# A two-layer decoder trunk with expert gathers: stream place in halves, VectorE work moved, two loads split by rows, fifteen tiny loads at the end

## What is computed

```python
def peer_ffn(h, w_q, sub_keys, u_tab, v_tab):
    q = (xt @ w_q).reshape(T, PEER_HEADS, 2, PEER_HALF)
    s = jnp.einsum('thpd,hpkd->thpk', q, sub_keys)
    s_top, i_top = lax.top_k(s, PEER_TOPK)              # 16 of 128, twice per head
    best, pos = lax.top_k(cand, PEER_TOPK)              # 16 of the 256 sums
    gates = jax.nn.softmax(best, axis=-1)
    act = jnp.einsum('chkd,cd->chk', u_tab[ib], xb)
    act = jax.nn.gelu(act) * gb
    return jnp.einsum('chk,chkd->cd', act, v_tab[ib])

for i in range(DEPTH):
    h = h + (diff_attention if i == 0 else short_conv)(rmsnorm(h, norm_mix[i]), ...)
    h = h + peer_ffn(rmsnorm(h, norm_ffn[i]), ...)
```

## Time and profile before

| | us |
|---|---|
| median of three runs | 1553.16 (1553.01 to 1554.8) |
| the profiled execution | 1554.41 |
| its span, first to last instruction | 1552.6 |
| TensorE busy | 1345.4 (87%) |
| VectorE busy | 1005.9 (65%) |
| ScalarE busy | 594.2 (38%) |
| GpSimd busy | 583.1 (38%) |
| moved by DMA | 626.06 MB, mean 403 GB/s |

### The profile page before, as it was taken

The page is one execution under the profiler, slowest core; times in us unless marked ns, Lnnn a source line. Parts: engine busy times, 40 slices in busy tenths (PEclk is TensorE's granted clock), DMA queues, the critical chain, the costliest instruction groups (busy, mean ns, idle before and its releaser), DMA issues.

```text
span 1552.6 us, 13146 instructions
## 1 busy us (share of the span) xinstructions
PE 1345.4 (87%) x3288; PEld 571.5 (37%) x3288; DVE 1005.9 (65%) x2452; ACT 594.2 (38%) x1809; POOL 583.1 (38%) x516
## 2 busy tenths in 40 slices
PE   8899898899868899988887889999888898777777
PEld 3454343344323443333332334344333333322222
DVE  5677877677566975445478636666548867765454
ACT  1334354534332444333334424343434344343333
POOL 0023334344323343333335444343344444444341
PEclk9999999999999999999999999999999999999999
DMA  9659999999999999999999999999999999999996
GB/s 395 247 230 418 419 415 414 420 365 420 418 422 419 372 418 420 418 421 420 419 420 420 417 421 421 420 419 420 420 417 389 423 421 421 421 421 422 420 422 281
DMA packets 92810, 626.06 MB, mean 403 GB/s; under 512 B 10304, under 2 KB 10432, under 8 KB 25152
## 3 DMA queue, kind: packets, MB, share of 16 engines
q0 software_dynamic: 73728, 536.90, 83.6%
q1 hardware_dynamic: 17280, 81.01, 12.9%
q10 hardware_dynamic: 1728, 7.31, 1.2%
HBM read 624.14 MB, written 1.05 MB: 403 GB/s over the span
## 4 chain that ended last, share of the span: by engine, by line
DMA 44%; PE 35%; DVE 12%; ACT 5%; issue 3%; POOL 0%; ACTq 0%; SPq 0%; DVEq 0%; POOLq 0%
DMA ring<-in_peer_uv_dram,idx 43%; PE acc L600 23%; PE pp L360 9%; DVE ring L1353 5%; ACT diag L915 1%; PE tt L375 1%; PE acc L360 1%; ACT weight L911 1%; DMA ring<-in_w_qkv_dram 1%; PE ss L434 1%; ACT gelu L909 1%; ACT L909 1%; ACT rows L737 1%; DVE mx L1022 0%; ACT L774 0%
## 5 line engine op out<-in xcount | busy, mean ns | idle before, releaser
L600 PE MATMUL acc<-ring,diag 128*128 128x512 f32 x2048 | 988.7, 609 | 153.0 <-ACT diag L915 142.3
L695 POOL DMA_INDIRECT ring<-in_peer_uv_dram,idx x512 | 582.9, 1139 | 948.8 <-PE acc L600 830.3
L1353 DVE CUSTOM_DVE_ANT_0 ring<-ring,xf 128x1024 f32<-128x1024 f32 x512 | 627.0, 1227 | 469.9 <-DMA ring<-in_peer_uv_dram,idx 459.0
L600 PEld LDWEIGHTS acc<-ring,diag 128*128 128x128 f32 x2048 | 372.1, 192 | 701.4 <-issue 688.4
L909 ACT ACTIVATE gelu<-dots 128x1 f32<-128x1 f32 x512 | 103.6, 202 | 816.9 <-DVE dots L1353 816.7
L915 ACT ACTIVATE diag<-const,weight 128x128 f32<-128x128 f32 x512 | 205.5, 401 | 17.2
L911 ACT ACTIVATE weight<-gelu,gates 128x1 f32<-128x1 f32 x512 | 150.7, 294 | 17.0
L360 PE MATMUL pp<-stream,xT 128*128 128x512 f32 x160 | 80.5, 593 | 0.0
L360 PE MATMUL pp<-stream,rows 128*128 128x512 f32 x128 | 65.9, 597 | 0.0
L360 PEld LDWEIGHTS pp<-stream,xT 128*128 128x128 f32 x160 | 30.2, 190 | 37.7 <-issue 37.7
L375 PE MATMUL tt<-const,rows 128*128 128x128 f32 x144 | 23.6, 287 | 21.5 <-ACT rows L708 15.7
(11 more groups left out here) (139 smaller groups left out, 746.9 us busy)
## 6 DMA issues: line engine op xcount, KB each, us to landing
stream<-in_peer_w_q_dram SPq DMA_DIRECT2D x36, 512.0 KB
stream<-in_conv_w_in_dram SPq DMA_DIRECT2D x32, 512.0 KB
stream<-in_w_qkv_dram SPq DMA_DIRECT2D x16, 512.0 KB
ring<-in_peer_uv_dram,idx POOLq DMA_INDIRECT x512
ring<-in_w_qkv_dram SPq DMA_DIRECT2D x3, 2048.0 KB, 24.2
stream<-in_w_o_dram SPq DMA_DIRECT2D x8, 512.0 KB
kept<-in_peer_w_q_dram SPq DMA_DIRECT2D x2, 2048.0 KB, 11.9
stream<-in_conv_w_out_dram SPq DMA_DIRECT2D x8, 512.0 KB
```

The costliest lines, as they stand in the source:

```text
L600: mm = nc.tensor.matmul(acc[half][:, :], diag[:, s % RING, :], row[:, D + half * 512:D + (half + 1) * 512], start=(k == 0), stop=(k == SLO ...
L695: nc.gpsimd.indirect_dma_start(dst, None, uv_dram, bass.IndirectOffsetOnAxis(idx[:, at:at + 1], 0)).then_inc(landed, 16)
L1353: nc.vector.tensor_tensor_reduce(row[:, 0:D], row[:, 0:D], xf[:, s // SLOTS % 2, :], 1.0, 0.0, ALU.mult, ALU.add, dots[:, s % RING:s % RIN ...
```

## The change

The stream place is filled in two halves of four k steps in place of four quarters of two. Of window 1's queries the third and fourth chunk are projected at slots 120 and 134 and not at 116 and 128; of window 0's the last at 51 and not 57; of window 3's the first at slot 88 of its count and not 90, and it is ranked one step a slot and not two. `scale_for_mixer` and `scale_for_experts` get a `yield` between the sum of squares and the root, with a tile of their own (`total`) for the sum, and the former starts four slots later. The two kept chunks named above are loaded as rows 0 to 119 and rows 120 to 127, and TensorE waits for both. Fifteen loads of i rows (i = 1 to 15) of 16 + i columns of the constants into a used part of `kept` are issued by SP after slot 506 has been used, ahead of its output stores, and waited for at the end.

```diff
@@ AT
-         wq0=94, wq1=104, wq2=116, wq3=128),
+         wq0=94, wq1=104, wq2=120, wq3=134),
@@
-         scale=86, wq0=90, wq1=106, wq2=132, wq3=156),
+         scale=86, wq0=88, wq1=106, wq2=132, wq3=156),
-LATE_RANK_PROJECT = {1: 0, 2: 25, 3: 57}
+LATE_RANK_PROJECT = {1: 0, 2: 25, 3: 51}
-RANK_PIECES = {(0, 1): 2, (0, 2): 2, (0, 3): 1, (1, 0): 2, (3, 0): 2}
+RANK_PIECES = {(0, 1): 2, (0, 2): 2, (0, 3): 1, (1, 0): 2}
-QUARTERS = 4
+FIFTEEN = {(2, "in", 2), (2, "out", 0)}
+MOST = 120
+PARTS = 2
+DEEP = KT // PARTS
@@ wait_weights
-                    if k % 2 == 0:
-                        pe.wait_ge(quarter_in[k // 2], 16 * (before + 1))
+                    if k % DEEP == 0:
+                        pe.wait_ge(part_in[k // DEEP], 16 * (before + 1))
                 elif k == 0:
                     pe.wait_ge(w_in[place], 16 * (before + 1))
+                    if (n, what, c) in FIFTEEN:
+                        pe.wait_ge(rest_in[(n, what, c)], 16)
@@ load_stream
-                size = KT // QUARTERS * CHUNK
-                for q in range(QUARTERS):
-                    if previous is not None and q < QUARTERS - 1:
-                        sp.wait_ge(quarter_used, (QUARTERS - 1) * (before - 1) + q + 1)
+                size = DEEP * CHUNK
+                for part in range(PARTS):
+                    if previous is not None and part < PARTS - 1:
+                        sp.wait_ge(part_used, (PARTS - 1) * (before - 1) + part + 1)
@@ the loads
+                    if (n, what, c) in FIFTEEN:
+                        sp.dma_start(places[place][0:MOST, :], matrix_of(n, what, c)[0:MOST, :]).then_inc(w_in[place], 16)
+                        sp.dma_start(places[place][MOST:P, :], matrix_of(n, what, c)[MOST:P, :]).then_inc(rest_in[(n, what, c)], 16)
+                    else:
+                        sp.dma_start(places[place], matrix_of(n, what, c)).then_inc(w_in[place], 16)
                 previous[place] = n, what, c
+            written(sp, pp, (3, "out", 0))
+            sp.wait_ge(v_used, ALL - 5)
+            for i in range(1, 16):
+                sp.dma_start(kept[0:i, 1, 64 * i:64 * i + 16 + i], consts[0:i, 0:16 + i]).then_inc(small_in[i - 1], 16)
             for b in range(2):
                 for c in range(2 - b):
                     sp.wait_ge(h_finished, 2 * (2 + b) + c + 1)
                     sp.dma_start(out_dram[b][:, c * CHUNK:(c + 1) * CHUNK], h[:, b, c * CHUNK:(c + 1) * CHUNK]).then_inc(out_done, 16)
+            for i in range(1, 16):
+                sp.wait_ge(small_in[i - 1], 16)
             sp.wait_ge(out_done, 64)
@@ scale_for_mixer, and the same in scale_for_experts
                 sum_squares(n % 2)
+                yield
                 rsqrt_of_mean(1, D, scale_mix[:, n:n + 1])
@@ output
                 yield at["scale"]
-                scale_for_experts(n)
+                yield from paced(scale_for_experts(n), at["scale"], 1)
@@ gated_input
-                yield at["x"]
-                scale_for_mixer(n)
+                yield at["x"] + 4
+                yield from paced(scale_for_mixer(n), at["x"] + 4, 1)
                 if n == 2:
-                    yield at["x"] + 2
+                    yield at["x"] + 7
```

More of the change, by code:

```diff
@@ L196, in build @@
         stat = sb("stat", [P, 8])
+        total = sb("total", [P, 1])
         root = sb("root", [P, 8])
@@ L228, in build @@
         w_first_in = [sem("w_first_in0"), sem("w_first_in1")]
-        quarter_in = [sem(f"quarter_in{i}") for i in range(QUARTERS)]
-        quarter_used = sem("quarter_used")
+        part_in = [sem(f"part_in{i}") for i in range(PARTS)]
+        part_used = sem("part_used")
+        rest_in = {(2, "in", 2): sem("rest_in0"), (2, "out", 0): sem("rest_in1")}
+        small_in = [sem("small_in%d" % i) for i in range(1, 16)]
         v_first_used = sem("v_first_used")
@@ L362, in project_part @@
                         mm.then_inc(pool.written_sem(key), 1)
-                    elif k % 2 and held(n, what, c)[0] == STREAM:
-                        mm.then_inc(quarter_used, 1)
+                    elif k % DEEP == DEEP - 1 and held(n, what, c)[0] == STREAM:
+                        mm.then_inc(part_used, 1)
             def project(pool, n, what, c, src, at, ks=range(KT)):
@@ L640, in load_stream @@
             def load_stream(n, what, c, before, previous):
-                size = KT // QUARTERS * CHUNK
-                for q in range(QUARTERS):
-                    if previous is not None and q < QUARTERS - 1:
-                        sp.wait_ge(quarter_used, (QUARTERS - 1) * (before - 1) + q + 1)
+                size = DEEP * CHUNK
+                for part in range(PARTS):
+                    if previous is not None and part < PARTS - 1:
+                        sp.wait_ge(part_used, (PARTS - 1) * (before - 1) + part + 1)
                     elif previous is not None:
                         written(sp, pp, last_reader(*previous))
-                    sp.dma_start(stream[:, q * size:(q + 1) * size],
-                                 matrix_of(n, what, c)[:, q * size:(q + 1) * size]).then_inc(quarter_in[q], 16)
+                    sp.dma_start(stream[:, part * size:(part + 1) * size],
+                                 matrix_of(n, what, c)[:, part * size:(part + 1) * size]).then_inc(part_in[part], 16)
             load_first()
@@ L661, in _ @@
                         written(sp, values_pool(1), (1, "values", 1))
-                    sp.dma_start(places[place], matrix_of(n, what, c)).then_inc(w_in[place], 16)
+                    if (n, what, c) in FIFTEEN:
[3 more added lines that the diff above has]
+                        sp.dma_start(places[place], matrix_of(n, what, c)).then_inc(w_in[place], 16)
                 previous[place] = n, what, c
+            written(sp, pp, (3, "out", 0))
+            sp.wait_ge(v_used, ALL - 5)
+            for i in range(1, 16):
+                sp.dma_start(kept[0:i, 1, 64 * i:64 * i + 16 + i], consts[0:i, 0:16 + i]).then_inc(small_in[i - 1], 16)
             for b in range(2):
@@ L940, in rsqrt_of_mean @@
             def rsqrt_of_mean(count, dim, y):
-                v, t = stat[:, 0:count], root_t[:, 0:count]
+                v, t = stat[:, 0:count] if count > 1 else total[:, :], root_t[:, 0:count]
                 link(nc.vector.tensor_scalar(v, v, 1.0 / dim, EPS, ALU.mult, ALU.add))
@@ L955, in sum_squares @@
             def sum_squares(b):
-                link(nc.vector.tensor_tensor_reduce(scratch[:, 0:D], h[:, b, :], h[:, b, :], 1.0, 0.0, ALU.mult, ALU.add, stat[:, 0:1]))
+                link(nc.vector.tensor_tensor_reduce(scratch[:, 0:D], h[:, b, :], h[:, b, :], 1.0, 0.0, ALU.mult, ALU.add, total[:, :]))
             def square_groups(src3, count, dim, sq):
@@ L1215, in front @@
                 dve.wait_ge(x_in[0], 16)
-                scale_for_mixer(0)
+                whole(scale_for_mixer(0))
                 prepare_gains()
@@ L1236, in front @@
                 dve.wait_ge(x_in[1], 16)
-                scale_for_mixer(1)
+                whole(scale_for_mixer(1))
                 add_output(0, 0)
                 add_output(0, 1)
-                scale_for_experts(0)
+                whole(scale_for_experts(0))
                 expert_rows(0)
```

## The result

The changed kernel takes 1566.48 us at the median (1565.17 to 1567.11) against 1553.54 for the kernel before in the same comparison: 1.0077 times as long, 95% interval 1.0064 to 1.0089. I had forecast 1543.5, and a range that ended at 1553. The change is slower by 13 us, and none of my rivals is the reason: that rival 2 names 1567 is chance, since its mechanism (late halves) is not what the trace shows.

What follows compares the result with a forecast made beforehand. The prediction took DMA transfers, 626 MB at 421 GB/s, plus idle time of the DMA engines as the bound. Terms -3 -3.5 -1 -1 +2 -2 -1.2 summed to -9.7 us, from 1553.16 to 1543.5 us; range 1535 to 1553.

Steps and rivals of the forecast that it cites:

- rival 2: Streamed halves land late where chunks' slots adjoin, so TensorE waits; 1567 us, or 1556 at 1 us each; chance 0.07.
- the first two dips: Transfer rate drops in slice 9 (365 GB/s, 5.1 us lost) and slice 14 (372 GB/s, 4.4 us lost).
- the third: Transfer rate drop in slice 31 (389 GB/s), 2.9 us lost.
- the tail: Last slots' loads from 1538 us: one of sixteen engines some 5 us behind, and every slot waits for it.
- (a): Streamed place in halves: 50 loads of 1 MB instead of 100 of 512 KB, -3 us (0 to -4.4).
- (b): VectorE in slots 129 to 136 (slice 14): scale split and later, rankings overlap less; -3.5 us (0 to -4.4).
- (e): TensorE in slots 134 to 141: late query projection beside the input chunk lengthens slots; +2 us (0 to +5).
- (c): Window 0's heads 6 and 7 projected at slot 51 instead of 57 (slice 9); -1 us (-5.1 to +3).
- (d): Window 3's first heads ranked one step a slot, project two slots earlier (slice 31); -1 us (0 to -2.9).
- (g): SP's end: window 2's two stores moved to the last slots, fifteen tiny issues hidden before the last store; -1.2 us.
- rival 3: SP's fifteen tiny issues hold up the last store; 1570 us at 2.35 us an issue; chance 0.04.
- (f): Two kept chunks loaded as 120 + 8 rows, sparing an engine that may be the lagging one; -2 us (-5 to +1.2).

Runs made afterwards that it cites:

- experiment 7: Changed kernel with whole kept loads, varied: streamed place in quarters 1550.12 us; steps at old slots, scales in one piece 1550.96; without tiny loads, stores early 1548.21, late 1547.54.
- experiment 6: Changed kernel with whole kept loads, its fifteen tiny loads replaced by five of 1, 2, 3, 8 and 16 rows, each followed by a marker load: 1546.23 us.

## Why the prediction was wrong, point by point

**What bounds the kernel: right.** What was won and lost stands in the GB/s lines: the first two dips gave some, the third and the tail nothing, and about half a rate for some 35 us was the place where the time was lost.

**(a) Halves: right in direction, the size within the noise.** Forecast -3, measured -3.0 with about 3 us of uncertainty. The rows of the kernel with whole loads show how: SP's queue takes 12.7% for 81.02 MB, 0.1567% a MB, where it was 0.1592%; the gathers have 0.1565%.

```profile
q0 software_dynamic: 73728, 536.90, 84.0%
q1 hardware_dynamic: 10320, 81.02, 12.7%
```

The packets say it more finely: from 120 to 1500 us, one of 4 KB on SP's queue took 0.163 us on average in the kernel before, and one of 8 KB 0.316 in this one, 3% less than two of the former. On the 52.4 MB streamed, 124 us at 421 GB/s, that is an estimate of some 3.6 us.

The shorter lead (rival 2) shows once, and costs next to nothing. The page's rows of the kernel before and of this one, busy us, mean ns, idle before:

```profile
L360 PE MATMUL pp<-stream,xT 128*128 128x512 f32 x160 | 80.5, 593 | 0.0
L368 PE MATMUL pp<-stream,xT 128*128 128x512 f32 x160 | 81.9, 602 | 4.1 <-issue 4.1
```

TensorE sat 4.1 us before one matmul on `stream`, at 1114.94, after window 3's first query chunk had moved two slots forward. The profile names nothing that it waited for; a half that had not landed would fit, since the wait is 2.3 us with quarters and gone at the old slots (experiment 7). Slices 29 and 30 have 421 and 414 GB/s, in the kernel before 420 and 417, so it hardly cost time. By my own sign (matmuls that wait for `stream`) it counts against the forecast that the loads stay hidden.

**(b) to (e), the moved steps: right in sum,** 3.5 forecast, 3.9 measured with about 3 us of uncertainty, and together only, since one run undid them all. In the page of the kernel with whole loads the slices read:

```profile
GB/s 396 248 215 421 421 411 415 421 379 421 421 423 421 397 421 420 421 422 421 421 422 420 421 422 421 422 412 422 421 414 421 395 405 420 421 421 422 421 422 307
```

Slice 9 went from 365 to 379, 14 of 420 over 38.7 us or 1.3 us, for (c)'s -1. That is no proof of (c): kernels without the move have 354 to 387 there, those with it 379 to 398, and none passes the 400 that I had named as its sign. Slice 14 went from 372 to 397, 2.3 us, which is (b) with (e) taken off; here the pages do not overlap (363 to 391 without the moves, 397 to 414 with them). The stall at `scale_for_mixer` is gone, and a smaller dip stands some 15 us behind it, where TensorE multiplies two chunks in the same slots. So (b)'s sign is met (every window of 2 us from 508 to 522 us has over 400 GB/s) and (e)'s, no new dip, is missed. In order of time, the two projections, from `kept` and from `spare`, lie between the slots' matmuls at 529.31 and 532.75, 3.44 us apart as forecast:

```profile
529.31 1.88 PE L608 MATMUL acc<-ring,diag 128*128 128x512 f32 x4
531.03 1.02 PE L368 MATMUL pp<-kept,xT 128*128 128x512 f32 x2
531.89 1.02 PE L368 MATMUL pp<-spare,rows 128*128 128x512 f32 x2
532.75 1.88 PE L608 MATMUL acc<-ring,diag 128*128 128x512 f32 x4
```

and the window of 2 us there is the dip's lowest:

```profile
532.00:534.00 2.00, 2.00 (x6) 0.84 (x5) 1.90 (x6) 1.76 (x6) 0.40 (x1) 1.00 0.84 258
```

(d) is not borne out: slices 32 and 33 have 395 and 405 where the earlier trace rows have 389 in slice 31. That dip moved and did not close.

**(g) The end: the issues are hidden, as forecast; the gain is not shown.** SP's fifteen issues took 6.77 us, 0.45 each, and were out by 1556.17. What SP's last store waits for, the first half of the last `finish`, came at 1561.85, so the store was not late (rival 3 falls). In the kernel after:

```profile
1549.40 6.77 SPq L679 DMA_DIRECT2D kept<-in_consts_dram  x15
...
1556.22 6.05 SPq L683 DMA_DIRECT2D out_dram<-h  x3
...
1561.16 0.69 DVE L1365 TENSOR_TENSOR h<-h,acc 128x512 f32<-128x512 f32 x1 [2.28 <-PE acc L608]
1562.02 0.69 DVE L1365 TENSOR_TENSOR h<-h,acc 128x512 f32<-128x512 f32 x1 [0.17 <-PE acc L608]
```

The 1.2 us is within what the runs can't tell.

**(f) 120 + 8 rows: the step that failed.** I put -2 us, bounded by -5 and +1.2; it cost 18 to 19. The bounds were wrong in kind. I asked only how many bytes each engine gets and took 26.3 GB/s an engine for each of them, the rate of gathers and loads of 128 rows, the only forms in the trace. That a form the trace does not have could move the same bytes slower was not in the bounds, nor that it would slow the gathers behind it. The row of the Trainium skill that the prediction set aside (DMA: Bandwidth & Descriptors, "Rules for kernel authors"), which wants one transfer of 128 partitions, pointed the right way, though it names no slower rate. That a load of 120 rows goes over fifteen engines agrees with the trace (at most fifteen rows in flight). The aim of the edit failed too: no time was won at the tail, where the kernel after still ends with one engine's rate,

```profile
1552.00:1554.00 2.00, 1.67 (x4) 0.68 (x4) 1.23 (x2) 0.46 (x3) 0.00 (x0) 1.00 0.12 42
1554.00:1556.00 2.00, 1.48 (x4) 0.68 (x4) 1.08 (x1) 0.63 (x2) 0.00 (x0) 1.00 0.09 27
```

as in the earlier trace rows. In experiment 6 an engine that serves the second row was late; whether the spared one was late too is not known.

Without (f) my sum is -7.7 us; the kernel with whole kept loads measured 0.995 of the kernel before, -7.8 (-5.3 to -10.4 by the interval). That the two agree to 0.1 us is luck: (d) shows no gain, and no single term is known to better than some 3 us. One term of seven decided the sign. My case for a slower kernel (0.12) sat on waits and issues, and none on a transfer that becomes slower by its shape.

## What to carry to other kernels

Before a load is cut by partitions, ask which doors each piece reaches, not how many engines it spares. In these runs pieces of 64 or 120 rows brought the whole traffic to about half its rate and pieces of sixteen to about a third (152 of 421 GB/s), gathers included, while a cut by columns (15 KB and 1 KB of each row) cost nothing. Where the trace has no row for the form of a transfer, the bound of its cost has to leave room for another rate on the same bytes. A DMA share near 1 with half the GB/s was the sign of it here; a dip with a low share, as in the earlier trace rows, was another matter, that of an engine which is late with its orders.

## What was not expected of the hardware

- Loads of 120 + 8 or 64 + 64 rows beside gathers: 210 to 229 GB/s in all, where 128 rows have 418 to 424; loads of sixteen rows: 152. The gathers' own packets go from 0.31 to about 0.60 us.
- Rows of 20 KB pitch in place of 16 KB change nothing in the 120 + 8 split (1572.18 us, one run, against 1572.42).
- A tiny load issued near the end landed 2.2 us later when it had two rows than with one: a late engine shows in the smallest load that uses it.
